# Weights of the first experts loaded during routing, and the last layer's expert rows added onto x in the output tensor

## The reference, cut to what matters

```python
h2 = modulate(rmsnorm(x, norm2_g[l]), sh2, sc2).reshape(bsz * L, d)
if last:
    y = moe_ffn(h2, router_w, router_b, w1[l], w3[l], w2[l])
    x = x + g2 * y.reshape(bsz, L, d)
...
# one block of up to 128 rows, all of one expert e
return (jax.nn.silu(xblk @ w1[e]) * (xblk @ w3[e])) @ w2[e]
# each row of a block, times its weight, is added to its token
out = jnp.zeros((n + 1, d), h.dtype).at[tok_buf].add(yb * w_buf[:, None])
```

## Time and profile before

| what | value |
|---|---|
| median of 3 runs | 3357.86 us (3352.55 to 3358.07) |
| the profiled execution | 3356.33 us |
| its span, first to last instruction | 3354.5 us |
| mean granted clock of TensorE | 0.965 of full |
| PE busy | 3135.0 us (93%) |
| DVE, ACT, POOL busy | 1628.8, 890.9, 767.6 us |
| moved by DMA | 518.23 MB, 154 GB/s over the span |

### The profile page before, as it was taken

How to read it: one execution, slowest core, us unless ns; L and a number is a source line. 1 busy time by engine, 2 the same in 40 slices (tenths; PEclk the granted TensorE clock), 3 DMA queues, 4 the chain that set the end, 5 groups by cost and what they waited for, 6 DMA issues and landing times. The chain is left out here.

```text
span 3354.5 us, 46133 instructions
## 1 busy us (share of the span) xinstructions
PE 3135.0 (93%) x15818; PEld 2404.5 (72%) x15819; DVE 1628.8 (49%) x2433; ACT 890.9 (27%) x1676; POOL 767.6 (23%) x494
## 2 busy tenths in 40 slices
PE   7999899999999978999999899899999996899995
PEld 5887577777777866676666788587777775566673
DVE  4562366666622565424553665265222256775512
ACT  4321265111112322222222321155211132122221
POOL 0140000110011225344343032000111123455441
PEclk9999899999999979999999899899999997999997
DMA  6122243334314228756786422142111333998764
GB/s 259 57 88 101 86 127 100 128 124 134 131 60 163 101 95 283 242 166 222 237 292 213 185 76 113 55 145 72 51 44 49 134 128 110 364 352 304 251 202 138
DMA packets 162584, 518.23 MB, mean 154 GB/s; under 512 B 30834, under 2 KB 81650, under 8 KB 138612
## 3 DMA queue, kind: packets, MB, share of 16 engines
q1 hardware_dynamic: 116080, 412.66, 33.1%
q0 software_dynamic: 17568, 59.82, 7.7%
q10 hardware_dynamic: 28804, 43.98, 4.3%
HBM read 430.90 MB, written 85.83 MB: 154 GB/s over the span
## 5 line engine op out<-in xcount | busy, mean ns | idle before, releaser
L218 PE MATMUL wide<-part,part 128*128 128x512 f32 (+2 forms) x2416 | 979.0, 405 | 40.2 <-DVE part L2550 17.5
L220 PE MATMUL wide<-part,part 128*128 128x512 f32 (+2 forms) x2416 | 932.8, 386 | 0.0
L219 PE MATMUL wide<-part,part 128*128 128x512 f32 (+2 forms) x2384 | 918.5, 385 | 0.0
L218 PEld LDWEIGHTS wide<-part,part 128*128 128x128 f32 x2416 | 460.7, 191 | 156.1 <-issue 66.0
L219 PEld LDWEIGHTS wide<-part,part 128*128 128x128 f32 x2384 | 455.2, 191 | 99.8 <-issue 17.7
L220 PEld LDWEIGHTS wide<-part,part 128*128 128x128 f32 x2416 | 459.9, 190 | 91.8
L2548 DVE CAST part<-place 128x2048 fp32r<-128x2048 f32 x128 | 183.8, 1436 | 434.1 <-DMA place<-in_w 428.4
L2415 PE MATMUL bank<-place,place 128*128 x832 | 370.2, 599 | 8.2 <-ACT place L2502 8.2
L1787 POOL TENSOR_TENSOR place<-place,place 128x512 f32 (+3 forms) x80 | 106.1, 1326 | 1088.6 <-DVE place L1751 1088.6
L2550 DVE TENSOR_TENSOR part<-place,part 128x2048 fp32r<-128x2048 f32 x128 | 314.5, 2457 | 4.4
L2415 PEld LDWEIGHTS bank<-place,place 128*128 128x128 f32 x832 | 155.8, 192 | 185.2 <-issue 185.2
(11 more groups left out here) (266 smaller groups left out, 3827.6 us busy)
## 6 DMA issues: line engine op xcount, KB each, us to landing
place<-in_w SPq DMA_DIRECT2D x124, 1024.0 KB, 15.2
place<-in_w SPq DMA_DIRECT2D x34, 2048.0 KB, 10.5
place<-in_ada_w ACTq DMA_DIRECT2D x72, 512.0 KB, 4.4
place<-in_w_gates SPq DMA_DIRECT2D x32, 640.0 KB, 4.5
place<-in_bias SPq DMA_DIRECT2D x96, 192.0 KB, 3.4
place<-in_ada_w SPq DMA_DIRECT2D x6, 2048.0 KB, 17.0
place<-in_w_rows SPq DMA_DIRECT2D x6, 2048.0 KB, 7.5
place<-in_w_gates SPq DMA_DIRECT2D x16, 768.0 KB, 4.5
```

The costliest lines, as they stand in the source:

```text
L218: pe.matmul(out, left[0], right[0], start=first, stop=False)
L219: pe.matmul(out, left[0], right[1], start=False, stop=False)
L220: return pe.matmul(out, left[1], right[0], start=False, stop=last)
```

## The change

It does four things.

1. During routing SP loads more. In the first layer w3 of expert 0 (2 MB) is issued ahead of the last tile's stores. In the last layer the slots are swapped (expert e takes slot (e + 1) % 2, `slot_of`), the load with tile 6 brings w1 of expert 1, and ahead of the last tile's stores all of w13 of expert 0 is loaded (4 MB), once the last w_o product is done. In `experts` SP then loads what is left of expert 1 and w2 of experts 0 and 1, in this order.
2. In the last layer x is stored to the output tensor instead of x_rows, the output gets TOK + P rows (the host takes the first 1024), and the adds go to it. acc isn't filled, x isn't loaded again, `combine` goes, and a stage `finish_adds` waits for the adds.
3. For that each block's rows have to be multiplied by g2 before they are added. PE and ACT spread g2 over the partitions at the start of the last layer's `experts` (PE waits for it ahead of its first `turn_slots`), and POOL multiplies each half of yb in `add_block`. To make room, gl takes the place of h3 in both layers, and ACT's copy of h3 also waits until the gated rows of the block before are turned.
4. In the last block of the first layer ACT copies the turned gated rows ahead of its load of tokens; in that of the last layer DVE copies them.

```diff
@@ mix_and_route, SP
             for t in range(NQ):
+                if t == NQ - 1:
+                    if last:
+                        sp.wait_ge(s_mm, 2 * NQ)
+                        sp.dma_start(w13[:, 1], s["a"]["w13"][layer, 0]).then_inc(s_w0, 16)
+                    else:
+                        sp.wait_ge(s_lg, 8)
+                        sp.dma_start(w13[:, 0, KD:], s["a"]["w13"][layer, 0, :, KD:]).then_inc(s_w0, 16)
                 sp.wait_ge(s_x, updated(t))
-                sp.dma_start(s["x_rows"][t * P:(t + 1) * P], X[t % 3]).then_inc(s_xst[t % 3], 16)
+                to = s["out"][0] if last else s["x_rows"]
+                sp.dma_start(to[t * P:(t + 1) * P], X[t % 3]).then_inc(s_xst[t % 3], 16)
...
-                    sp.dma_start(first_w1, s["a"]["w13"][layer, 0, :, 0:KD]).then_inc(s_w1, 16)
+                    sp.dma_start(w13[:, 0, 0:KD], s["a"]["w13"][layer, int(last), :, 0:KD]).then_inc(s_w1, 16)
             sp.wait_ge(s_w1, 16)
+            sp.wait_ge(s_w0, 16)
@@ experts
+    gl = h3
+    g2 = [place(at + 2 * DE, DE), place(A_W13 + 40960, DE)]
...
+    def slot_of(e):
+        return (e + last) % 2
+    def loaded_ahead(e, i):
+        return e == 0 or last and e == 1 and i < PIECES // 2
@@ experts, SP
             for e in range(EXP):
-                b = e % 2
+                b = slot_of(e)
...
+                if e == 1:
+                    for q in range(2):
+                        sp.wait_ge(s_xb[q], 16)
                 for i in range(PIECES):
-                    if e == 0 and i < PIECES // 2:
-                        sp.sem_inc(s_w13[0][i], 16)
+                    if loaded_ahead(e, i):
+                        sp.sem_inc(s_w13[b][i], 16)
                         continue
...
+                if e == 1:
+                    load_w2(0)
...
+                if e >= 1:
+                    load_w2(e)
...
@@ experts, PE
+            if last:
+                for h in range(2):
+                    cols = [s["mod"][:, layer, 5 * KD + 4 * h + j, 0:1] for j in range(4)]
+                    broadcast_columns(s, pe, cols, banks[6 + h]).then_inc(s_g2, 1)
+                pe.wait_ge(s_g2c, 2)
             for n in range(2):
                 turn_slots(0, n, n)
@@ experts, ACT
             def copy_h3(n):
                 act.wait_ge(s_h3, n + 2)
                 act.wait_ge(s_g, n + 1)
+                act.wait_ge(s_tg, n + 1)
...
             R = act.snap(used // 2)
+            if not last:
+                copy_gated(R, 0)
             load_to_add(R, 0)
-            copy_gated(R, 0)
             copy_y(R, 0)
@@ experts, DVE
             dve.wait_ge(s_split, (EXP + 2) * PIECES)
+            if last:
+                used = dve.value_load(plan[0:1, PLAN_USED:PLAN_USED + 1], min_val=1, max_val=MAXB)
+                dve.wait_ge(s_tg, used // 2 * 2 + 2)
+                apart(dve, s_tail)
+                dve.tensor_copy(gt.rearrange("p a b -> p (a b)"), banks[4][:]).then_inc(s_gc, 1)
@@ experts, POOL
             def add_block(r, b):
-                pool.wait_ge(s_yc, r * 4 + (2 * b + 4))
+                if last:
+                    pool.wait_ge(s_g2c, 2)
+                    for h in range(2):
+                        pool.wait_ge(s_yc, r * 4 + (2 * b + h + 3))
+                        apart(pool, s_pass)
+                        y = yb[b][:, h * 512:(h + 1) * 512]
+                        pool.tensor_tensor(y, y, g2[h], ALU.mult).then_inc(s_yg, 1)
+                    pool.wait_ge(s_yg, r * 4 + (2 * b + 2))
+                else:
+                    pool.wait_ge(s_yc, r * 4 + (2 * b + 4))
                 pool.wait_ge(s_add, r * 32 + (16 * b + 32))
@@ the last stage: combine goes, finish_adds comes, its SP alone does something
             s["clear_last"](sp)
             used = sp.value_load(s["plan"][0:1, PLAN_USED:PLAN_USED + 1], min_val=1, max_val=48)
             sp.wait_ge(s["y_added"], used // 2 * 32 + 48)
             apart(sp, s_go)
```

More of the change, by code:

```diff
@@ L188, in hybrid_backbone @@
                             experts)]
-        stages.append((combine, (DEPTH - 1, True)))
+        stages.append((finish_adds, (DEPTH - 1, True)))
         for n, (stage, args) in enumerate(stages):
@@ L1862, in mix_and_route @@
     s_sent, s_zero, s_w1 = s["pool_dma_sem"]("tokens_sent"), sem("no_tokens_before"), sem("w1_loaded")
-    first_w1 = place(A_W13, 2, 2 * KD, DE)[:, 0, 0:KD]
+    w13 = place(A_W13, 2, 2 * KD, DE)
+    s_w0 = sem("w13_loaded")
     broadcasts = [(v, w, h) for v in range(3) for w in range(NW) for h in range(2)]
@@ L2355, in _ @@
                 sp.sem_inc(s_room, 1)
-            sp.wait_ge(s_ahead[0], 16)
+                sp.wait_ge(s_ahead[0], 16)
             for b in range(2):
@@ L2422, in body @@
                               for b in range(3)]
-                slots = [pe.snap(e % 2, min_val=0, max_val=1) for e in experts_of]
+                slots = [pe.snap(slot_of(e), min_val=0, max_val=1) for e in experts_of]
                 for b in range(2):
@@ L2468, in _ @@
             act.sem_inc(s_xh, 4)
+            act.sem_inc(s_tg, 1)
+            if last:
+                for h in range(2):
+                    act.wait_ge(s_g2, h + 1)
+                    act.activation(g2[h], banks[6 + h][:], ACT.Copy).then_inc(s_g2c, 1)
             def copy_turned(half, b, n):
@@ L2542, in _ @@
             with dve.Fori(0, EXP - 1, 2) as e:
-                for b in range(2):
+                for n in range(2):
+                    b = slot_of(n)
                     for i in range(PIECES):
@@ L2599, in add_rows @@
             def add_rows(b):
-                pool.indirect_dma_start(out=s["acc"], out_offset=bass.IndirectOffsetOnAxis(toadd[b][:, 0:1], 0),
+                pool.indirect_dma_start(out=s["out"][0] if last else s["acc"],
+                                        out_offset=bass.IndirectOffsetOnAxis(toadd[b][:, 0:1], 0),
                                         in_=yb[b], in_offset=None, compute_op=ALU.add).then_inc(s_add, 16)
@@ L2636, in _, with finish_adds @@
             add_block(pool.snap(used // 2), 0)
[L2639 to L2667 removed]
+def finish_adds(s, layer, last):
+    nc = s["nc"]
+    s_go = s["sem"]("adds_passed")
+    with nc.Block() as block:
         @block.sync
@@ L2674, in _ @@
             apart(sp, s_go)
-            for t in range(NTX):
-                sp.dma_start(Y[:, t], s["acc"][t * P:(t + 1) * P]).then_inc(s_y[t], 16)
-            for t in range(NTX):
-                sp.wait_ge(s_x, t + 1)
-                sp.dma_start(s["out"][0][t * P:(t + 1) * P], X[:, t]).then_inc(s_out, 16)
-            sp.wait_ge(s_out, 16 * NTX)
 def _constants():
```

67 lines of the change are left out of this document (22 added, 45 removed).

## The result

The changed kernel takes 3334.52 us (median of 5 runs, 3324.85 to 3339.78), the kernel before beside it 3355.39 (5 runs, 3352.55 to 3358.07): ratio 0.9936, 95% interval 0.9917 to 0.9954. It is faster, by 21 us where 43 to 44 were forecast. The measured time lies outside the forecast's range of 3304 to 3321.

The account below looks back on a forecast made before the run. PE bounds nearly all the time, so savings count only at both experts starts and the end: 26.0 + 4.5 + 10.5 + 3.0 + 0.4 = 44.4 us off 3356.33, forecast 3312; 8-in-10 range 3304 to 3321.

Parts of the forecast that it names:

- End of the program and last block, 26.0 + 4.5: Program end: dropping combine saves 26.0 us; last block: DVE's earlier copy and faster w2 matmuls, less POOL's multiplication, save 4.5.
- The 46 multiplications on POOL ... nobody waits for that inside the loop: Last layer's loop: multiplications by g2 take 2.9 us per 19 us block, delay an add about 1.5 us, cost nothing.
- the first rival: Saturated stretch: POOL's multiplications hold up splits PE waits for; 29 us lost (3341), more likely 7 (3319); chance 0.13.
- The rule of the Trainium skill: VectorE and GpSimd share SBUF ports, held for a whole instruction, so each multiplication meeting a split delays it its full length.
- The last layer's start, 10.5: Last layer's experts: earlier weights remove PE's waits of 1.29, 0.44 and most of 9.17 us, plus 1.4 of clock: 10.5 us.
- The first layer's start and end, 3.0 + 0.4: First layer's experts: waits of 2.50 and 0.46 us go at the start; ACT copies 0.45 us earlier at the end.
- The 4 MB in routing, the spread of g2, adds to the output: Routing, last layer's start and adds: these edits cost nothing, covered by other work, PE's idling or equal transfers.
- routing gets longer: Routing: the 4 MB load delays last stores or token table beyond 17 us of cover, say 8 us: 3320; chance 0.04.
- the saturated stretch gains too: Last layer, five 20.0 us blocks: an earlier start lets weights get ahead, 4.2 us more gained: 3308; chance 0.08.
- The narrow range, 3306 to 3318: Whole program: the forecast's own range, from end 24 to 28, clock 2.7 and base 1.5 us; forecast's chance 0.60.
- the clock's 2.7 us: Last block: after a shorter gap PE's 16 w2 matmuls take 7.03 us, not 9.71, saving 2.7; otherwise the block gives 1.8.

Follow-up runs that it names:

- e1: Changed kernel without POOL's 46 multiplications by g2 (result leaves out g2 in the last layer): 3321.22 us, ratio 0.9898 to the kernel before.
- e3: Changed kernel's output side alone, with the loads, slots and SP's order of the kernel before: 3338.37 us, ratio 0.9944 to the kernel before.
- e8: Changed kernel, multiplications kept, loading only half of each w2 from expert 2 of the last layer on: 3313.25 us (one run).
- e11: Changed kernel with SP issuing up-weights of expert e ahead of down-weights of e-1, both layers, same bytes: 3312.32 us, ratio 0.9875 to the kernel before.
- e6: Changed kernel, block 0's gate between the zero adds, DVE's fourth piece split only after POOL's two subtractions for block 0: 3322.68 us, 0.9904 to the kernel before.
- e2: Changed kernel's early loads, swapped slots and earlier last-block copies, with combine, acc and load of x as before: 3343.91 us, ratio 0.9967 to the kernel before.

## Why the prediction was wrong

Its steps, one by one:

- **End of the program and last block, 26.0 + 4.5.** Right, and in its parts: 30.6 measured. The gap ahead of PE is 1.24 us (about 1.0 said) and its matmuls take 7.13 (7.03 said); POOL's last multiplication takes 1.26 (1.4 said).
- **"The 46 multiplications on POOL ... nobody waits for that inside the loop", priced at nothing. This is the step that failed most.** It asked who waits for a multiplication, and that is indeed nobody. It did not ask what the multiplication does to the splits that PE waits for. Taken out, they give back 14.1 us (233.1 to 219.0). The mechanism stood in the text as the first rival, with 0.13 and prices of 7 and 29 us; the measured price is in the middle. The rule of the Trainium skill that the prediction set against the change was the right one, and the reason given against it, that DVE is only 76 of 105 us busy, was the wrong reading: DVE's idle time was waiting for late weights, and PE stood waiting for its split already before, 1.9 us of 105. Shown by e1, e3, e8 and e11.
- **The last layer's start, 10.5.** 3.6 measured at s2. The waits on DVE went as said (1.29, 0.44 and 9.17 are gone), but two others took their place: POOL's subtractions, stretched by the splits that now never pause (2.89 us at PE), and the gate behind the second zero add (3.49 us). The step asked what is late next and looked only at the weights. With both mended (e6) the start is 53.7 us, 13.7 under before: the time was there to be had, but not by the loads alone.
- **The first layer's start and end, 3.0 + 0.4.** The start is 1.1 us longer instead, by the same two waits (2.89 and 2.27 us at PE). e6 shows 552.5 us from plan to last silu, 7.0 under before. The end gained more than was said: from the last silu to ACT's first copy for the next stage it was 28.9 us and is 27.4, 1.5 less, since ACT comes to the copy of the gated rows after 1.39 us of "issue" and not 2.68.
- **The 4 MB in routing, the spread of g2, adds to the output.** Nothing lost, as said: PE turns its first gathered rows 11.3 us behind the plan in both kernels, the saturated stretch of e2 (217.3 us) is that of before (218.0), and from the first layer's last silu to the second plan no kernel takes longer than the one before (1018.9 us). So the rival "routing gets longer" fell away as well.
- **The rival "the saturated stretch gains too", 4.2 us.** Not in after. By e11's 210.7 us, blocks 2 to 13 had 218.0 - 210.7 = 7.3 us to give even in the kernel before, by an order that the change didn't touch; that order wasn't run on the kernel before.
- **The narrow range, 3306 to 3318.** Its low end doesn't follow from its terms: the clock's 2.7 us can only be lost, so they give 3308.5.

In numbers, for the profiled executions: the forecast asked for 44.4 us, 16.5 came, so 27.9 are missing. 15.1 were lost in blocks 2 to 13, 6.9 at the last start, 4.1 in the first layer up to its last silu, and its end gave 1.1 back; the rest, 2.9, lies in the stretches that vary from run to run.

## What to carry to other kernels

"Nobody waits for this instruction" isn't the end of the question: ask also which engine's instruction it makes longer, and whether somebody waits for that one. An engine with a quarter of its time idle has no slack if its idle time is all ahead of late data; look at the wait behind the data, not at the busy share. And where a load queue stands in a wait, see whether the loads behind it could already go: putting them in the order in which the consumer frees their slots gave blocks 2 to 13 as much here (210.7 us) as leaving out the multiplications and a sixth of the weights together.

## What the runs showed that was not expected

- DVE's subtraction and a two-input operation of POOL exclude each other almost exactly in three places: 2.29 + 2.80 us against 5.07 measured (after), 2.29 + 2.77 against 5.05 (after, first layer), 2.29 + 1.54 against 3.80 (e11 at 2914). Two subtractions of POOL took 5.49 us beside uninterrupted splits.
- An add of 128 rows (512 KB) to DRAM landed 17.05 us after its issue while weights streamed (the chain of waits of after, below), so that one zero add behind another holds up what POOL has queued.
- A DMA share of 0.98 at 363 GB/s looked like a bound. It was not: while each block has its own expert, e11 has a share of 1.01 at 382 GB/s, and e8, with fewer bytes, 0.92 at 325, and both are faster. Why a share near 1 stands for different rates isn't shown.

```profile
2854.89 17.05 DMA out_x<-place,toadd
```
